# The decay rows of a state-space branch in two row groups of TensorE, and four products of a constant tile at its start

## The chip, the cores and the metric

The kernel runs on one core of a Trainium2 chip. The metric is the device time of one execution in microseconds; three timed runs and one profiled execution of the kernel before are at hand. Everything is computed in fp32.

## The reference, cut to what matters

A first block (state-space mixer and differential attention side by side, then a convolutional feed-forward) is followed by a second block of two layers. Each layer of the second block normalizes its input, projects it, sends slices of the projection through four branches and projects their joined outputs back. One of the four branches is a state-space model with a scalar decay for each of four heads:

```python
def ssd_branch(xbc, dt_raw, z, conv_w, conv_b, dt_bias, a_log, d_skip, norm_g):
    ...
    dt = jax.nn.softplus(dt_raw.astype(f32) + dt_bias.astype(f32))
    a = (dt * (-jnp.exp(a_log.astype(f32)))).reshape(bsz, nc, CHUNK, C_GROUPS, e)
    ...
    a_cs = jnp.cumsum(a, axis=2)
    xdt = xs * dt[..., None]
    ...
    seg = a_cs[:, :, :, None] - a_cs[:, :, None, :]
    lmat = masked_exp(causal, seg)
    cb = jnp.einsum('bclgn,bcsgn->bclsg', cm, bm)
    scores = cb[..., None] * lmat
    y_diag = jnp.einsum('bclsge,bcsgep->bclgep', scores, xdt)
    wx = xdt * jnp.exp(a_cs[:, :, -1:] - a_cs)[..., None]
    states = jnp.einsum('bclgn,bclgep->bcgepn', bm, wx)
    ...
```

`dt` and the running sum `a_cs` are thus four rows (one for a head) of 512 positions. Each has to be spread over 128 partitions, since it multiplies whole tiles. The first thing that the whole program does is the norm of the first block: the sum of squares over 1024 channels for each of 528 positions, in two halves of 264.

## The kernel before, in words

The kernel is one hand-written program: each engine has its instruction list in the order in which it runs, and the engines wait for each other by semaphores. Activations lie with channels on partitions and positions along the free dimension. Weights stream through a ring of four slots of 512 KB (`ring`), loaded by SyncE as slots become free. PSUM has eight banks, `bank(0)` to `bank(7)`; in the second block `take(b)` lets PE wait until bank b was released, and `full(b)` on ScalarE or `got(b)` on VectorE waits until it was written.

**The start.** ScalarE squares the input channel tile by tile (L1477). PE sums the squares over partitions by products with a matrix of ones (`norm_sum`, L491): four tiles alone, and one tile into which VectorE has added the other four (`squares_half`, L2233). ScalarE makes the inverse root (L1479, L1480), VectorE scales the input with it (`norm_half`, L2241), and each scaled tile releases a product of the first projection (`proj_half`, L510). The order on PE is norm_sum(0), proj_half(0, 0), proj_half(1, 0), norm_sum(1), and so on. VectorE writes some small constants at its start (L2190 to L2193); the last of these raises `eps_ready`, for which ScalarE waits before its first table load (L1455). PE waits only for its constants (`ones_in`, L500) and its data.

**The decay rows.** One weight slot of each layer, `misc`, has the four columns for `dt` in columns 0 to 3. So the projection leaves `dt_raw` on partitions 0 to 3 of a tile. VectorE adds the bias and takes the absolute value (L2785, L2786), ScalarE does exponential and logarithm (L1903 to L1905), VectorE finishes the softplus, multiplies by the decay rate and takes the running sum (L2793 to L2796). The results are `DT4`, which is `POSF[0:4]`, and `AC4`, which is `R[0:4]`. All of that runs early in the layer.

**Spreading them.** Much later in the layer, behind the last attention head, comes this order on PE (L1322 on): `c_decay`, `late(22, 0, 1)`, `c_cols`, `b_states`, `c_turn(10)`, `late(22, 2, 3)`, `c_turn(12)` and so on. `c_decay` makes four products, one for a head, with `sel4` as the stationary operand: four rows, of which one is 1, so that row h of `AC4` comes out on all 128 partitions of bank 2 + h. ScalarE turns each bank into two tiles and a column (L2004 to L2006). `c_cols` transposes the four rows of `DT4` and `AC4`, eight tiles of 4 x 128 into one bank, and ScalarE copies the 32 columns (L2009); VectorE needs them in `c_seg` (L3001). `late(j, x)` (L969) is a part of a projection: four products of 256 columns for each x, into one of two banks.

In the trace each fp32 product is two records of weight load and two of product.

Of the kernel before, what the change touches and what calls it, by code (L numbers as in the profile page):

```python
# [69 lines left out]
BANK = {name: i % 4 for i, name in enumerate(PHASE1)}  # L70
BANK |= {"km": 1, "k1": 3, "nk2": 2, "nk3": 3, "y0": 0, "y1": 3, "y2": 3, "y3": 3}

MAGIC = 12582912.0
# [76 lines left out]
def build(nc, a, out):  # L150

    with ExitStack() as ctx:
# [200 lines left out]
        KRR = R[:, 0:SEQ]  # L353
        AC4 = R[0:4, 0:SEQ]
        DT4 = POSF[0:4, :]
        ACB, EAB, DD = QF, SD, QF
# [28 lines left out]
        def bank(b):  # L385

            return PS[b // 2][:, b % 2, :]
# [73 lines left out]
        def _(pe):  # L461
# [33 lines left out]
            def chunk_in(b):  # L495

                s, value = n.now("hn_ready")
                pe.wait_ge(s, value - (KD - 1 - b))

            pe.wait_ge(SEMS["ones_in"], 16)  # L500

# [36 lines left out]
            def s5_out(a):  # L538
# [8 lines left out]
                ins.then_inc(SEMS[f"act_full{p}"], 1)  # L547

            norm_sum(0)
            proj_half(0, 0)  # L550
            proj_half(1, 0)
# [379 lines left out]
            for l in range(LAYERS):  # L931
# [211 lines left out]
                def c_decay():  # L1143
                    pe.wait_ge(*n("c_mul"))
                    for h in range(4):
                        take(2 + h)
                        mm(bank(2 + h), c("sel4", h * P, P, 4), AC4[0:4, :], start=True, stop=True).then_inc(SEMS[f"ba{2 + h}"], 1)

                def c_cols():
                    take(7)  # L1150
                    for t in range(4):
                        for x in range(2):
                            ins = nc.tensor.transpose(bank(7)[:, t * 8 + 4 * x:t * 8 + 4 * x + 4], (DT4, AC4)[x][0:4, t * P:t * P + P],
                                                      c("ident", 0, 4, 4))
                    ins.then_inc(SEMS["ba7"], 1)
# [282 lines left out]
        def _(act):  # L1438
# [338 lines left out]
            for l in range(LAYERS):  # L1777
# [124 lines left out]
                act.wait_ge(*n("c_dve"))  # L1902
                step(af(R[0:4, 0:SEQ], R[0:4, 0:SEQ], ACT.Exp, scale=-1.0))  # L1903
                af(LB2[0:4, 0:1], v2(l, "alog", rows=4), ACT.Exp)
                af(R[0:4, 0:SEQ], R[0:4, 0:SEQ], ACT.Ln, bias=epsc[0:4, 2:3]).then_inc(SEMS["c_act"], 1)  # L1905
                swapped()
# [101 lines left out]
                full(7)  # L2008
                released(af(COL.rearrange("p a b -> p (a b)"), bank(7)[:, 0:32], ACT.Copy), 7)  # L2009
                mark("c_acb")  # L2010
# [158 lines left out]
        def _(dve):  # L2169
# [17 lines left out]
            def join():  # L2187
                link(dve.drain())

            v.memset(epsc[:, 0:1], EPS)  # L2190
            v.memset(epsc[:, 1:2], 1e-5)
# [586 lines left out]
            for l in range(LAYERS):  # L2778
# [5 lines left out]
                dve.wait_ge(*n("d_misc"))  # L2784
                link(ts(DT4, PJ2[0:4, 16, :], v2(l, "dtb", rows=4), None, ALU.add))  # L2785
                stt(R[0:4, 0:SEQ], DT4, -1.0, DT4, ALU.mult, ALU.max).then_inc(SEMS["c_dve"], 1)  # L2786
                dve.wait_ge(*n("d_root"))
# [4 lines left out]
                dve.wait_ge(*n("c_act"))  # L2792
                link(stt(DT4, DT4, 0.0, R[0:4, 0:SEQ], ALU.max, ALU.add))  # L2793
                link(ts(LB2[0:4, 0:1], LB2[0:4, 0:1], -1.0, None, ALU.mult))
                link(ts(AC4, DT4, LB2[0:4, 0:1], None, ALU.mult))
                v.tensor_tensor_scan(AC4, c("keep", 0, SEQ, 4), AC4, 0.0, ALU.mult, ALU.add).then_inc(SEMS["c_mul"], 1)  # L2796

# [477 lines left out]
def layout(x):  # L3275
# [20 lines left out]
    for l in range(LAYERS):  # L3296
        w2 = f["w_in_2"][l]
        two = lambda o: [chunks(w2, s) for s in slices(o, 2)]
        misc = np.zeros((D, P), np.float32)
        misc[:, 0:4] = w2[:, c0 + 768:c0 + 772]  # L3300
        misc[:, 64:96] = w2[:, c0 + 1412:c0 + 1444]
        misc[:, 96:128] = misc[:, 64:96][:, swap]
        slots += two(c0 + 1028) + [chunks(w2, slice(c0 + 1284, c0 + 1412)), chunks(misc, slice(0, P))]
        for o in (0, 256, P, 256 + P):
            slots.append(chunks(w2, slice(o, o + P)))
        for o in (3 * 256 + 256, 3 * 256, 3 * 256 + 512):
            slots += two(o)
        slots += [chunks(w2, s) for s in slices(c0, 6)]
        for o in (c0 + 772, c0 + 1444, 6 * 256, 512):
            slots += two(o)  # L3310
        wo2 = f["w_out_2"][l].reshape(4, 256, D)[[2, 0, 1, 3]].reshape(D, D)
        slots += [chunks(wo2, s) for s in slices(0, 8)]
# [14 lines left out]
    def cols(v):  # L3327
        return v.reshape(-1, P).T
# [14 lines left out]
    for k in range(4):  # L3343
        sel4[k, k] = 1.0
    invf = np.zeros((P, 1))
# [4 lines left out]
    for i in range(4):  # L3350
        for q in range(64):
            b, m = q >> i, 1 << i
            lvl[2 * m * b:2 * m * b + m, i, q] = 1.0
    small, par2 = [], []
    for l in range(LAYERS):
        qb = f["d_qb_w_2"][l].reshape(2, P, 4, QKR)
# [6 lines left out]
            "lbl": cols(f["b_lb_logits_2"].reshape(-1)), "bng": cols(f["b_norm_g_2"][l]), "ccw": cols(f["c_conv_w_2"][l].reshape(-1)),  # L3363
            "ccb": cols(f["c_conv_b_2"][l]), "dtb": f["c_dt_bias_2"][l][:, None], "alog": f["c_a_log_2"][l][:, None],
            "dsk": cols(np.repeat(f["c_d_2"][l], 64)), "cng": cols(f["c_norm_g_2"][l]), "qag": cols(f["d_qa_g_2"][l]),
# [30 lines left out]
```

## Time and profile before

| | |
|---|---|
| timed runs | 1502.93, 1503.41, 1507.72 us; median 1503.41 |
| the profiled execution's own time | 1503.56 us |
| its span, first to last instruction | 1501.80 us |
| mean granted clock of TensorE | 0.996 |
| PE busy / weight loads / VectorE / ScalarE / GpSimd | 98% / 73% / 63% / 30% / 6% of the span |
| chain that ended last, by engine | PE 89%, VectorE 8%, issue 1% |
| DMA | 120.10 MB, mean 80 GB/s |

The page gives busy time by engine, the span in slices, the chain of work that ended last (followed back from the last instruction, at each step to what released it) and the costliest groups of instructions. Narrower views list instructions in order of time, the busy time of each engine in a chosen stretch with the granted clock, or one source line. A busy share says nothing by itself where stages have different limits, so the stretches that the change touches are looked at alone.

### The profile page before, as it was taken

To read this page: it belongs to the slowest core of one execution; us is meant where nothing else is said; L and a number is where in the kernel's file an instruction comes from. 1 tells how busy PE (TensorE), PEld (TensorE's weight loads), DVE (VectorE), ACT (ScalarE), POOL (GpSimd) and SP (SyncE) were. 2 spreads that over 40 slices of the span, in tenths; PEclk is the share of its full clock that TensorE was granted. 3 is DMA by queue.
4 is the path that set the end of the run, shared out by engine and by line. 5 is a ranking of instruction groups with operands and counts; after the bars stand their busy time and mean duration, and the time that the engine had idled before them with its cause. 6 is when DMAs were issued, how large, how long until landed. Compare 5 with 4: busy or idle time off the path is not lost.

```text
span 1501.8 us, 18758 instructions
## 1 busy us (share of the span) xinstructions
PE 1472.8 (98%) x7228; PEld 1091.7 (73%) x7228; DVE 952.9 (63%) x1657; ACT 449.3 (30%) x929; POOL 97.2 (6%) x70
## 2 busy tenths in 40 slices
PE   7999999999999999999999999999999999999997
PEld 6886777888888888888888844555867745456855
DVE  5849476623777666777634268877743577876833
ACT  3674444530121111111100242134443342243432
POOL 0252000000000000000000051000000150000000
PEclk9999999999999999999999999999999999999999
DMA  5211111142212222222222321112132311111132
GB/s 215 84 43 57 57 57 57 57 164 80 75 69 97 84 84 85 84 85 84 87 96 98 113 70 57 57 43 84 43 127 71 127 47 65 45 54 43 57 126 70
DMA packets 38297, 120.10 MB, mean 80 GB/s; under 512 B 4000, under 2 KB 8352, under 8 KB 37696
## 3 DMA queue, kind: packets, MB, share of 16 engines
q1 hardware_dynamic: 37872, 116.66, 22.9%
q0 software_dynamic: 336, 2.23, 0.4%
q8 instruction: 58, 0.95, 0.3%
q14 instruction: 31, 0.25, 0.1%
HBM read 112.58 MB, written 6.29 MB: 79 GB/s over the span
## 4 chain that ended last, share of the span: by engine, by line
PE 89%; DVE 8%; issue 1%; DVEq 1%; DMA 0%; ACT 0%; SPq 0%; ACTq 0%
PE PS L844 19%; PE PS L941 14%; PE PS L911 9%; PE PS L969 5%; PE PS L521 5%; PE PS L664 5%; PE PS L1217 4%; PE PS L788 4%; PE PS L1360 4%; PE PS L1387 3%; PE PS L510 2%; PE PS L620 2%; DVE SC L2804 1%; PE PS L1018 1%; PE PS L758 1%
## 5 line engine op out<-in xcount | busy, mean ns | idle before, releaser
L941 PE MATMUL PS<-HN,ring 128*128 128x512 f32 x576 | 258.0, 595 | 0.0
L941 PEld LDWEIGHTS PS<-HN,ring 128*128 128x128 f32 x576 | 107.0, 190 | 121.1 <-issue 118.8
L844 PE MATMUL PS<-SC 128*128 128x257 f32 x624 | 144.1, 380 | 3.6 <-DVEq L2185 3.5
L1722 ACT ACTIVATE SC<-PS 128x257 f32<-128x257 f32 x60 | 23.1, 385 | 374.8 <-PE PS L844 296.6
L844 PEld LDWEIGHTS PS<-SC 128*128 128x128 f32 x624 | 118.1, 190 | 21.8 <-DVEq L2185 4.8
L2804 DVE SCALAR_TENSOR_TENSOR SC<-SC 128x512 f32<-128x512 f32 x120 | 109.7, 914 | 5.4
L844 PE MATMUL PS<-HN,ring 128*128 128x257 f32 x352 | 79.8, 380 | 0.0
L844 PEld LDWEIGHTS PS<-HN,ring 128*128 128x128 f32 x352 | 66.8, 190 | 9.5
L521 PE MATMUL PS<-HN,ring 128*128 128x257 f32 (+1 forms) x320 | 71.6, 383 | 0.0
L521 PEld LDWEIGHTS PS<-HN,ring 128*128 128x128 f32 x320 | 60.4, 190 | 10.1 <-issue 1.1
L1217 PE MATMUL PS<-HN,ring 128*128 128x256 f32 x256 | 56.4, 380 | 0.0
L1387 PE MATMUL PS<-PJ,ring 128*128 128x256 f32 (+2 forms) x256 | 56.2, 380 | 0.0
L788 PE MATMUL PS<-PJ,ring 128*128 128x257 f32 x256 | 55.6, 380 | 0.0
L2493 DVE TENSOR_TENSOR SC<-ring 128x512 f32<-128x512 f32 x37 | 25.6, 693 | 47.2 <-DMA ring<-wst 41.2
L1360 PE MATMUL PS<-PJ,ring 128*128 128x512 f32 x128 | 55.3, 592 | 0.0
L911 PE MATMUL PS<-PJ,SC 128*128 128x256 f32 x240 | 54.7, 379 | 0.0
L1217 PEld LDWEIGHTS PS<-HN,ring 128*128 128x128 f32 x256 | 48.5, 190 | 7.2 <-issue 0.7
L788 PEld LDWEIGHTS PS<-PJ,ring 128*128 128x128 f32 x256 | 48.5, 190 | 6.9
L1387 PEld LDWEIGHTS PS<-PJ,ring 128*128 128x128 f32 x256 | 43.9, 190 | 13.0 <-issue 1.0
L911 PEld LDWEIGHTS PS<-PJ,SC 128*128 128x128 f32 x240 | 45.6, 190 | 6.2
L844 PE MATMUL PS<-SC,ring 128*128 128x257 f32 x208 | 49.4, 379 | 0.0
L3195 DVE TENSOR_TENSOR PJ<-PJ 128x512 f32<-128x512 f32 (+3 forms) x18 | 9.2, 514 | 62.5 <-ACT PJ L2058 62.3
(563 smaller groups left out, 2667.7 us busy)
## 6 DMA issues: line engine op xcount, KB each, us to landing
ring<-wst SPq DMA_DIRECT2D x188, 512.0 KB, 3.7
outT<-X SPq DMA_DIRECT2D x18, 256.0 KB, 4.4
X<-xT SPq DMA_DIRECT2D x16, 264.0 KB, 5.5
X<-outT SPq DMA_DIRECT2D x16, 256.0 KB, 4.8
V<-small POOLq DMA_DIRECT2D x2, 1024.0 KB, 6.6
outT<-X SPq DMA_DIRECT2D x4, 384.0 KB, 2.6
V<-s5w SPq DMA_DIRECT2D x1, 1280.0 KB, 10.5
consts<-cst SPq DMA_DIRECT2D x1, 1235.5 KB, 12.9
```

The source lines that it names most:

```text
L510: ins = mm(PS[p][:, h, 0:H], ring[:, j, b * P:b * P + P], HN[:, b, HX[h]], start=(b == 0), stop=(b == KD - 1))
L521: ins = mm(PS[p][:, h, 0:q.stop - q.start], ring[:, k % 4, b * P:b * P + P], HN[:, b, q], start=(b == 0), stop=(b == KD - 1))
L664: ins = mm(PS[at % 2][:, 1, 0:257], left[:, b * P:b * P + P], right[:, b, :], start=(b == 0), stop=(b == 3))
L788: ins = mm(PS[p][:, h, 0:257], ring[:, s, (4 * x + b) * P:(4 * x + b) * P + P], src, start=(b == 0), stop=(b == 3))
L844: ins = mm(PS[at % 8 // 2][:, at % 2, 0:257], left[:, b * P:b * P + P], right[:, b, :], start=(b == 0), stop=(b == 3))
L911: ins = mm(PS[at % 8 // 2][:, at % 2, 0:256], left, right, start=(b == 0), stop=(b == KH - 1))
L941: ins = mm(bank(b), ring[:, r, i * P:i * P + P], HN[:, i, 0:SEQ], start=(i == 0), stop=(i == KD - 1))
L969: ins = mm(bank(b)[:, 0:256], left[x][:, k * P:k * P + P], right[x][:, k, :], start=(k == 0), stop=(k == 3))
L1217: ins = mm(bank(in_bank(l, j))[:, 0:256], ring[:, j, x * P:x * P + P], HN[:, x, HF[h]], start=(x == 0), stop=(x == KD - 1))
L1360: ins = mm(bank(out_bank(l, i)), ring[:, j % WSLOTS, b * P:b * P + P], PJ2[:, src, :], start=(x == 0), stop=(x == KD - 1))
L1387: ins = mm(bank(out_bank(l, i))[:, 0:q.stop - q.start], ring[:, j % WSLOTS, b * P:b * P + P], PJ2[:, src, q], start=(x == 0), stop=(x == K ...
L2804: link(stt(CA[:, cc, :], x, w1, CA[:, cc, :], ALU.mult, ALU.add))
```

## The change

Four things are done.

- `sel4`, the `dt` columns of `misc`, the bias and the decay rate are laid out so that the four heads lie on rows 0, 1, 32 and 33 (`DTROW`) instead of 0 to 3; `DT4` and `AC4` have 34 rows, of which 30 hold zeros or values that nobody uses. The operations of VectorE and ScalarE on them take 34 partitions.
- `c_decay` goes through the heads in the order 0, 2, 1, 3. Each product takes two rows, 0-1 for heads 0 and 1 and 32-33 for heads 2 and 3.
- `c_cols` transposes tiles of 34 x 128 with a 34 x 34 identity; ScalarE picks the eight wanted columns of each head pair in two copies.
- VectorE first fills 512 columns of a tile with 1.0. PE, as soon as `eps_ready` is raised, multiplies that tile with itself three times (128 x 128 by 128 x 512, into bank 7, nobody reads it) before it waits for its constants, and once more between norm_sum(0) and proj_half(0, 0).

```diff
+DTROW = [0, 1, 32, 33]
+NDT = 34
...
-        AC4 = R[0:4, 0:SEQ]
-        DT4 = POSF[0:4, :]
+        AC4 = R[0:NDT, 0:SEQ]
+        DT4 = POSF[0:NDT, :]
...
+            pe.wait_ge(SEMS["eps_ready"], 1)
+            for _ in range(3):
+                mm(PS[3][:, 1, :], BB[:, 0, 0, :], BB[:, 0, 0:4, :], start=True, stop=True)
             pe.wait_ge(SEMS["ones_in"], 16)
...
+            def warm(n_):
+
+                for _ in range(n_):
+                    mm(PS[3][:, 1, :], BB[:, 0, 0, :], BB[:, 0, 0:4, :], start=True, stop=True)
+
             norm_sum(0)
+            warm(1)
             proj_half(0, 0)
...
                 def c_decay():
                     pe.wait_ge(*n("c_mul"))
-                    for h in range(4):
+                    for h in (0, 2, 1, 3):
                         take(2 + h)
-                        mm(bank(2 + h), c("sel4", h * P, P, 4), AC4[0:4, :], start=True, stop=True).then_inc(SEMS[f"ba{2 + h}"], 1)
+                        rows = slice(32 * (h // 2), 32 * (h // 2) + 2)
+                        s0 = CC["sel4"][0] + h * P
+                        mm(bank(2 + h), cst[rows, s0:s0 + P], AC4[rows, :], start=True, stop=True).then_inc(SEMS[f"ba{2 + h}"], 1)
 
                 def c_cols():
                     take(7)
                     for t in range(4):
                         for x in range(2):
-                            ins = nc.tensor.transpose(bank(7)[:, t * 8 + 4 * x:t * 8 + 4 * x + 4], (DT4, AC4)[x][0:4, t * P:t * P + P],
-                                                      c("ident", 0, 4, 4))
+                            o = (2 * t + x) * NDT
+                            ins = nc.tensor.transpose(bank(7)[:, o:o + NDT], (DT4, AC4)[x][:, t * P:t * P + P], c("ident", 0, NDT, NDT))
                     ins.then_inc(SEMS["ba7"], 1)
...
-                step(af(R[0:4, 0:SEQ], R[0:4, 0:SEQ], ACT.Exp, scale=-1.0))
-                af(LB2[0:4, 0:1], v2(l, "alog", rows=4), ACT.Exp)
-                af(R[0:4, 0:SEQ], R[0:4, 0:SEQ], ACT.Ln, bias=epsc[0:4, 2:3]).then_inc(SEMS["c_act"], 1)
+                step(af(AC4, AC4, ACT.Exp, scale=-1.0))
+                af(LB2[0:NDT, 0:1], v2(l, "alog", rows=NDT), ACT.Exp)
+                af(AC4, AC4, ACT.Ln, bias=epsc[0:NDT, 2:3]).then_inc(SEMS["c_act"], 1)
...
-                released(af(COL.rearrange("p a b -> p (a b)"), bank(7)[:, 0:32], ACT.Copy), 7)
+                for g in range(2):
+                    ins = af(COL.rearrange("p t (x h) -> p (t x) h", x=2)[:, :, 2 * g:2 * g + 2],
+                             bank(7)[:, 0:8 * NDT].rearrange("p (a b) -> p a b", b=NDT)[:, :, 32 * g:32 * g + 2], ACT.Copy)
+                released(ins, 7)
...
+            v.memset(XS.rearrange("p a r n -> p (a r n)")[:, 0:512], 1.0)
             v.memset(epsc[:, 0:1], EPS)
...
-                link(ts(DT4, PJ2[0:4, 16, :], v2(l, "dtb", rows=4), None, ALU.add))
-                stt(R[0:4, 0:SEQ], DT4, -1.0, DT4, ALU.mult, ALU.max).then_inc(SEMS["c_dve"], 1)
+                link(ts(DT4, PJ2[0:NDT, 16, :], v2(l, "dtb", rows=NDT), None, ALU.add))
+                stt(AC4, DT4, -1.0, DT4, ALU.mult, ALU.max).then_inc(SEMS["c_dve"], 1)
...
-                link(ts(AC4, DT4, LB2[0:4, 0:1], None, ALU.mult))
-                v.tensor_tensor_scan(AC4, c("keep", 0, SEQ, 4), AC4, 0.0, ALU.mult, ALU.add).then_inc(SEMS["c_mul"], 1)
+                link(ts(AC4, DT4, LB2[0:NDT, 0:1], None, ALU.mult))
+                v.tensor_tensor_scan(AC4, c("keep", 0, SEQ, NDT), AC4, 0.0, ALU.mult, ALU.add).then_inc(SEMS["c_mul"], 1)
...
-        misc[:, 0:4] = w2[:, c0 + 768:c0 + 772]
+        misc[:, DTROW] = w2[:, c0 + 768:c0 + 772]
...
-        sel4[k, k] = 1.0
+        sel4[DTROW[k], k] = 1.0
```

## Rows read from the trace of the kernel before

**Rows 1.** The page, part 4: the chain that ended last, by engine.
```profile
PE 89%; DVE 8%; issue 1%; DVEq 1%; DMA 0%; ACT 0%; SPq 0%; ACTq 0%
```

**Rows 2.** Stretches: us, busy time (instructions) of PE, PEld, DVE, ACT, POOL; clock; DMA.
```profile
1044.20:1047.80 3.60, 3.60 (x9) 1.40 (x8) 1.13 (x2) 3.37 (x9) 0.00 (x0) 1.00 0.27 112
...
1048.70:1052.10 3.40, 3.40 (x10) 2.66 (x9) 0.00 (x0) 1.63 (x5) 0.00 (x0) 0.50 0.46 154
...
1379.80:1383.20 3.40, 3.40 (x10) 2.69 (x9) 0.00 (x0) 1.83 (x6) 0.00 (x0) 0.50 0.47 154
...
1291.10:1294.50 3.40, 1.79 (x6) 0.51 (x5) 3.12 (x8) 1.99 (x5) 0.00 (x0) 1.00 0.01 2
...
318.90:321.70 2.80, 2.80 (x21) 2.20 (x21) 0.69 (x1) 2.38 (x6) 0.00 (x0) 1.00 0.32 126
```

**Rows 3.** The chain of waits, 1030 to 1075 us: start, us, what.
```profile
1044.30 3.62 PE PS L1147 x8
1047.93 5.34 PE PS L969 x16
1053.26 0.59 PE PS L1153 x8
...
1055.72 3.46 PE PS L969 x16
1059.18 0.87 PE PS L1162 x8
```

**Rows 4.** The start in order of time: start, us, instruction, count [idle before, releaser].
```profile
3.82 0.21 ACT L1473 ACTIVATE SC<-params 128x16 f32<-128x16 f32 x1 [1.55 <-DMA params<-par]
...
6.70 4.62 PE L491 MATMUL PS<-HN,consts 128*128 128x264 f32 x10 [6.70 <-ACT HN L1477]
...
10.03 0.66 PEld L491 LDWEIGHTS PS<-HN,consts 128*128 128x128 f32 x2 [0.22 <-DVEq L2185]
...
10.69 0.60 DVE L2215 SCALAR_TENSOR_TENSOR SC<-SC 128x16 f32<-128x16 f32 x3
...
13.09 7.14 PE L510 MATMUL PS<-HN,ring 128*128 128x264 f32 x31 [1.76 <-DVE HN L2241]
...
20.28 2.39 PE L491 MATMUL PS<-HN,consts 128*128 128x264 f32 x10
```

**Rows 5.** PE in order of time, 186 to 194 us, attention scores of the first block.
```profile
186.90 0.60 PE L689 MATMUL PS<-PJ 64*128 64x400 f32 x1
186.90 0.60 PE L691 MATMUL PS<-PJ 64*128 64x400 f32 x1
...
187.77 2.00 PE L664 MATMUL PS<-X,SC 128*128 128x257 f32 x8
...
192.79 0.69 PE L684 MATMUL PS<-PJ 64*128 64x512 f32 x1
...
193.32 0.59 PE L684 MATMUL PS<-PJ 64*128 64x512 f32 x1
```

**Rows 6.** VectorE in order of time: the running sum in layer 0.
```profile
884.68 1.21 DVE L2796 TENSOR_TENSOR_SCAN R<-consts,R 4x512 f32<-4x512 f32 x1
```

**Rows 7.** ScalarE and VectorE in order of time, behind the decay products of layer 0.
```profile
1053.89 0.20 ACT L2009 ACTIVATE SC<-PS 128x32 f32<-128x32 f32 x1 [0.20 <-PE PS L1153]
...
1054.75 0.29 DVE L2872 COPY SC<-PS 128x128 f32<-128x128 f32 x1 [9.38 <-PE PS L1095]
...
1060.21 0.18 DVE L3001 TENSOR_TENSOR SC<-SC 128x16 f32<-128x16 f32 x1
```

**Rows 8.** VectorE in order of time: a one-input operation on 512 columns.
```profile
52.43 0.43 DVE L2304 TENSOR_SCALAR SC<-SC 128x512 f32<-128x512 f32 x1
```

**Rows 9.** The line of the weight loads, 0 to 14 us.
```profile
L417 SPq DMA_DIRECT2D ring<-wst x4: 467/656/706, 3.7 to 8.8; - x4
...
DMA to landing us min/median/max: 6.4/7.5/8.1
```

**Rows 10.** PE in order of time: the transposes ahead of the output projections, first block.
```profile
318.93 3.02 PE L771 MATMUL PS<-consts,SC 2*128 2x2 f32 x20
```

More of the change, by code:

```diff
@@ L2792, in _ @@
                 dve.wait_ge(*n("c_act"))
-                link(stt(DT4, DT4, 0.0, R[0:4, 0:SEQ], ALU.max, ALU.add))
-                link(ts(LB2[0:4, 0:1], LB2[0:4, 0:1], -1.0, None, ALU.mult))
-                link(ts(AC4, DT4, LB2[0:4, 0:1], None, ALU.mult))
-                v.tensor_tensor_scan(AC4, c("keep", 0, SEQ, 4), AC4, 0.0, ALU.mult, ALU.add).then_inc(SEMS["c_mul"], 1)
+                link(stt(DT4, DT4, 0.0, AC4, ALU.max, ALU.add))
+                link(ts(LB2[0:NDT, 0:1], LB2[0:NDT, 0:1], -1.0, None, ALU.mult))
+                link(ts(AC4, DT4, LB2[0:NDT, 0:1], None, ALU.mult))
+                v.tensor_tensor_scan(AC4, c("keep", 0, SEQ, NDT), AC4, 0.0, ALU.mult, ALU.add).then_inc(SEMS["c_mul"], 1)
                 def taps(cc, lo, hi):
@@ L3354, in layout, with at_rows @@
     small, par2 = [], []
+    def at_rows(v):
+        out = np.zeros((NDT, 1), np.float32)
+        out[DTROW, 0] = v
+        return out
     for l in range(LAYERS):
@@ L3363, in layout @@
             "lbl": cols(f["b_lb_logits_2"].reshape(-1)), "bng": cols(f["b_norm_g_2"][l]), "ccw": cols(f["c_conv_w_2"][l].reshape(-1)),
-            "ccb": cols(f["c_conv_b_2"][l]), "dtb": f["c_dt_bias_2"][l][:, None], "alog": f["c_a_log_2"][l][:, None],
+            "ccb": cols(f["c_conv_b_2"][l]), "dtb": at_rows(f["c_dt_bias_2"][l]), "alog": at_rows(f["c_a_log_2"][l]),
             "dsk": cols(np.repeat(f["c_d_2"][l], 64)), "cng": cols(f["c_norm_g_2"][l]), "qag": cols(f["d_qa_g_2"][l]),
```

## The prediction, made before the changed kernel was run

> **What bounds the kernel now.** I read the page first: the chain that ended last is 89% PE [rows 1]. So a microsecond counts only if it is taken out of PE's own queue, or out of one of the few waits of PE. The change touches two places, and I read a narrower view of each.
>
> The first is the decay products (L1147), once in each of the two layers of the second block. In the table by stretches [rows 2] PE is never idle there, and the granted clock falls right behind them: 1.00 during the decay products, then 0.50 (the 1.2 GHz level of the two) from 1048.7 to 1052.1. The same comes in layer 1 at 1379.8. What the engine did before each fall is the same: products that fill 4 of 128 rows. In the chain [rows 3] the eight records take 3.62 us, and the sixteen records behind them (the first two `late` products) 5.34 us, where sixteen of the same size take 3.46 us at 1055.72.
>
> The second is the start [rows 4]. The ten records of the first norm sum (L491) take 4.62 us from 6.70; the same ten take 2.39 us at 20.28. That isn't ScalarE's pace alone: the last product of the first group has its input at 10.03 and ends at 11.32. So PE is at the lower level there (0.44 us a record against 0.22); the clock's own records begin only later. ScalarE's root, VectorE's scaling and the first projection (13.09) follow that end.
>
> **The change, part by part.** All sums are against the profiled execution: 1503.56 us, a span of 1501.80 and 1.76 around it; the median of the runs is 1503.41, 0.15 less.
>
> *Decay products, two row groups.* Today eight records follow each other at 0.43 to 0.45; in the chain up to the next product it is 3.62 us [rows 3]. After the change head 0 sits on rows 0-1 and head 2 on rows 32-33, in different banks, then 1 and 3. The kernel has such pairs already: the attention scores of the first block (L689 and L691) use rows 0-63 and 64-127. Both start at 186.90 and the next product starts at 187.77 [rows 5]: two 400-column products in 0.87 us, though one 512-column product alone takes about 0.9 (two records, [rows 3]). So pairs overlap, with a wait on a bank between them too. A 512-column product of such a pair has its two records 0.53 apart (192.79, 193.32), not 0.43: I take it that the second weight load is no longer hidden. Four steps of 0.53 are 2.12, so a gain of 3.62 - 2.12 = 1.5 us a layer, **3.0 us**. Ends: four steps of 0.43 (1.72 us, gain 1.9 a layer); or eight steps of 0.53 without overlap (4.24, a loss of 0.6 a layer). I take the pair's own row because it is the same size and mode. The Trainium skill (TensorE: Matmul & The Clock Gate, Part 3, Measured speedup vs the span model) has packed tiles last as long as one product plus about 4 ns a tile; by that the four products would take two product lengths, about 1.72 us, and the time would be 0.8 us lower than mine. The 0.53 of rows 5 speaks for the longer value.
>
> *The clock behind them.* With the four products down to 2.1 us I expect no fall. 3.4 us at half clock cost 1.7 us a layer [rows 2], so **3.4 us** in all; ends 0 and the whole difference of rows 3, 5.34 - 3.46 = 1.88 a layer. What speaks for it: from 1291.1 to 1294.5 PE is busy for 1.79 of 3.40 us, so it stands still for 1.6, and the clock stays at 1.00 [rows 2]. A mostly empty array for 2.1 us is only a little more than that, so this is the least certain term.
>
> *Transposes of 34 instead of 4 rows* (c_cols). The eight take 0.59 us a layer; eight with 128 columns take 0.87 [rows 3]. Between 0 and 0.28, nearer to the small end: 0.1 a layer, **+0.2 us**.
>
> *ScalarE and VectorE.* Operations on 34 partitions instead of 4 have the same number of columns; I cost them at nothing, and the last of them (the scan, L2796) is done at 885.9 in layer 0, 158 us ahead of the products that use it [rows 6]. The copy of the columns (L2009) becomes two of 0.20 us. Its reader on VectorE comes 6.1 us later (1060.21 against 1054.09, [rows 7]), so that is covered; without the cover it would cost 0.2 a layer. The zero columns of the projection and the tables change no DMA. Reordering the four `take` waits costs nothing: in the chain PE passes all four without a gap [rows 3].
>
> *The start.* VectorE's memset of 128x512 stands ahead of `eps_ready`, for which ScalarE waits, and now PE. Nothing in the trace is that memset; a 128x512 tensor_scalar takes 0.43 [rows 8], so `eps_ready` comes 0.4 later, at about 1.4. ScalarE hides that: it is done with its table load 1.55 us before the parameters land [rows 4]. So does VectorE, whose next operation waits for the same transfer. Three 512-column products at the low level are six records of 0.44 x 512/264 = 0.85, so 5.1 us, from 1.5 to 6.6 at the latest; the first real product starts at 6.70. The cover is thin, but 0.2 us late there would cost nothing, since the sum waits for its last input until 10.03. With the clock up, that last product runs from 10.06 and ends after 0.22 + 0.39 at 10.67 instead of 11.32: **0.65 us**. VectorE is free for the scaling at 11.29 (L2215, [rows 4]), and the first weights are there by about 10.1 (issued at 3.7, 6.4 to landing, [rows 9]), so the first projection can start at 12.4. The fourth product (`warm(1)`, 0.86 us) then runs from 10.5 to 11.4, inside PE's wait for VectorE. Ends: 0 where the clock comes up too late, 0.65.
>
> *Sum:* 0.65 + 3.0 + 3.4 - 0.2 = 6.85; 1503.56 - 6.85 = **1496.7 us**, 0.45% below the median. Behind the decay, VectorE idles 9.4 us until b_states [rows 7] and moves with PE; what could be late next is ScalarE, which copies the decay banks that PE takes again in c_turn, but that is two `late` products and some transposes further on, over 5 us of PE. About 0.3% (4.5 us) is what a measurement of this kernel can tell from no change.
>
> **The rivals.**
> 1. *The clock still falls behind the shorter decay products, in both layers.* For it: 2.1 us of two or four rows is still a stretch in which the array is nearly empty, and six transposes stand just ahead. Against it: it is 1.5 us shorter, and two groups work at a time. 1496.7 + 3.4 = 1500.1. The Trainium skill (same page, Part 4: PE-mode transpose) says that transposes don't count as busy for the clock in the same way, which would make the weak stretch longer. By that 1500.1 would be the likelier; but from 318.9 to 321.7 PE does twenty transposes (L771) and nothing else to speak of, and the clock stays at 1.00 [rows 2, 10]. Chance 0.16.
> 2. *One fall is left, or a new one comes.* After the change the sum's early products take 0.22 a record, so PE idles between them and until 10.03, and it can drop to the low level as the projections begin; the wait at 1291 also meets the clock at another moment. A fall costs 1.7: 1498.4. Against it: the waits of 1.76 us ahead of 13.09 and of 1.6 at 1291 left the clock up [rows 2, 4]. Chance 0.13.
> 3. *The groups take turns* (slower): each weight load waits for the other group's product, no overlap, eight steps of 0.53. That is 0.6 a layer more, and the clock falls as now: 1503.56 + 1.2 + 0.2 - 0.65 = 1504.3; with a fall twice as long, 1507.7. The whole is slower than before as soon as the products of a layer take over 3.85 us (3.62 + half of 0.65 - 0.1) with the clock as now. Against it: rows 5. Chance 0.05.
> 4. *The change doesn't do what it says:* the four products run one after the other as now, and only the start gains: 1503.1. Chance 0.04.
>
> **How the numbers follow.** The forecast has 0.62. The range goes from 1495.2 (1.9 and 1.88 a layer for the two decay terms, no charge for the transposes, and the 0.15 by which the median lies below the profiled execution) to 1501.0 (rival 1 with nothing gained at the start and the transposes at their upper end). It leaves out rivals 3 and 4. Faster by over 0.3% (below 1498.9) is the forecast and most of rival 2: 0.72. Slower by over 0.3% is rival 3 with the longer fall and what I have not seen: 0.03. The rest, 0.25, is within 0.3%.
>
> **What would show it.** In the profile after: the eight records of the decay products within about 2.1 us and starting in pairs; the granted clock 1.00 in the stretch behind them, and its sixteen records in some 3.5 us; the last record of the first norm sum ending at about 10.7 and the first projection starting at about 12.4. The forecast is wrong if the clock still reads 0.50 behind the decay, if the pair's records follow each other, or if the first projections run at 0.44 a record.

## The result, and the profile of the changed kernel

**Faster, and by more than forecast.** The changed kernel's median is 1495.28 us over four executions (1494.77 to 1495.38). The kernel before, run beside it, gave 1504.39 (1502.93 to 1507.72). The ratio is 0.9938, 95% interval 0.9924 to 0.9953. On the median of 1503.41 that I was shown this is 1494.1 us, or 9.3 us less, where the forecast had 6.85. A second set of executions gave 1494.96 us and the same ratio [0.9926, 0.9950]. One thing stands out before any view is opened: the kernel before spreads over 5 us, the changed one over 0.6.

First the page of the changed kernel: its span, and the chain by engine, which answers to [rows 1].

```profile
span 1493.0 us, 18777 instructions
...
PE 90%; DVE 8%; issue 1%; DVEq 1%; DMA 0%; ACT 0%; SPq 0%; ACTq 0%
```

PE is still nearly the whole chain. The span is 8.8 us shorter than the 1501.80 of before. Next the table by stretches, with the columns of [rows 2]: the decay products and the two `late` products behind them, first in layer 0, then in layer 1.

```profile
1042.50:1044.46 1.96, 1.96 (x10) 0.68 (x8) 1.14 (x2) 1.73 (x5) 0.00 (x0) 1.00 0.54 226
1044.46:1048.11 3.65, 3.65 (x18) 2.96 (x16) 0.00 (x0) 3.65 (x12) 0.00 (x0) 1.00 0.41 140
1369.66:1371.60 1.94, 1.94 (x10) 0.69 (x9) 1.12 (x2) 1.71 (x5) 0.00 (x0) 1.00 0.00 0
1371.60:1375.25 3.65, 3.65 (x19) 2.96 (x17) 0.00 (x0) 3.65 (x12) 0.00 (x0) 1.00 0.44 146
```

The granted clock is 1.00 in all four; before it was 0.50 behind the decay products of both layers. The chain of waits of the changed kernel gives the lengths, as [rows 3] did.

```profile
1042.62 1.92 PE PS L1161 x8
1044.53 3.65 PE PS L981 x16
1048.18 0.62 PE PS L1168 x8
...
1050.67 3.46 PE PS L981 x16
1054.13 0.87 PE PS L1176 x8
```

Line by line against [rows 3]: the decay products (now L1161) take 1.92 instead of 3.62 us, the sixteen `late` records (L981) 3.65 instead of 5.34, the eight transposes (L1168) 0.62 instead of 0.59. The rows below them are unchanged. Last the start in order of time, as in [rows 4].

```profile
0.92 0.48 DVE L2207 MEMSET SC<- 128x512 f32 x1 [0.92 <-PEq L3413]
...
1.50 5.49 PE L505 MATMUL PS<-SC 128*128 128x512 f32 x6 [1.50 <-DVE junk L2211]
6.78 2.41 PE L494 MATMUL PS<-HN,consts 128*128 128x264 f32 x8
9.44 0.71 PE L494 MATMUL PS<-HN,consts 128*128 128x264 f32 x2 [0.25 <-DVEq L2202]
9.98 1.02 PE L558 MATMUL PS<-SC 128*128 128x512 f32 x2
11.91 2.46 PE L516 MATMUL PS<-HN,ring 128*128 128x264 f32 x10 [0.91 <-DVE HN L2259]
...
5.57 2.18 ACT L1491 ACTIVATE HN<-X 128x264 f32<-128x264 f32 x6 [1.54 <-DMA X<-xT]
```

The three early products fill 1.50 to 6.99, the fourth (L558) fills half of PE's wait, and the first projection (L516) starts at 11.91 instead of 13.09. Not all of these 1.18 us are the change's: the last row shows that the first input tile reached ScalarE at 5.57, where the profiled execution of before had 6.13. A second profile of the changed kernel (below) has 6.08 there and is the fairer one to compare.

I went along PE's instructions one by one and noted how far each is ahead of the same one before. The gains named so far came where I looked for them, but there are three more steps, of 0.13, 0.36 and 0.33 us, at 213, 439 and 1294 us, where the change touches nothing. The two larger ones come out of VectorE (so does the smallest: ahead of L2365 at 210.75 us it idled 0.52 us in the kernel before, 0.15 in the changed one). Its rows in order of time, the kernel before:

```profile
424.30 0.42 DVE L2561 SCALAR_TENSOR_TENSOR X<-PS,X 128x257 f32<-128x257 f32 x1 [0.71 <-PE PS L844]
...
1281.46 1.23 DVE L2840 TENSOR_TENSOR PJ<-PJ,SC 128x1024 f32<-128x1024 f32 x1 [0.50 <-DVE SC L2838]
...
1293.76 0.52 PE L1027 MATMUL PS<-consts,SC 128*128 128x128 f32 x3 [1.39 <-ACT PJ L1840]
```

The same instructions in the changed kernel:

```profile
422.63 0.42 DVE L2579 SCALAR_TENSOR_TENSOR X<-PS,X 128x257 f32<-128x257 f32 x1 [0.35 <-PE PS L856]
...
1276.05 1.23 DVE L2858 TENSOR_TENSOR PJ<-PJ,SC 128x1024 f32<-128x1024 f32 x1
...
1288.34 0.52 PE L1039 MATMUL PS<-consts,SC 128*128 128x128 f32 x3 [1.02 <-ACT PJ L1854]
```

Twice 0.36 us of idle time is gone from VectorE, and the chain VectorE, ScalarE, PE hands the second on: PE waits 1.02 instead of 1.39 us at L1027 of before. The experiments had to tell whether this belongs to the change or to one execution.

### The profile page after: what moved, and what is told of

Same layout as the page of the kernel before. It is cut to its first block, busy times and chain, and to the rows that moved or that the text cites. A ratio compares the mean times of both kernels' runs of the same rounds, so it can differ in the third digit from the quotient of the medians.

```text
span 1493.0 us, 18777 instructions
## 1 busy us (share of the span) xinstructions
PE 1470.7 (99%) x7236; PEld 1089.3 (73%) x7236; DVE 952.7 (64%) x1658; ACT 448.9 (30%) x931; POOL 97.1 (7%) x70
## 4 chain that ended last, share of the span: by engine, by line
PE 90%; DVE 8%; issue 1%; DVEq 1%; DMA 0%; ACT 0%; SPq 0%; ACTq 0%
PE PS L856 19%; PE PS L953 14%; PE PS L923 9%; PE PS L981 5%; PE PS L676 5%; PE PS L527 5%; PE PS L1231 4%; PE PS L800 4%; PE PS L1374 4%; PE PS L1401 3%; PE PS L516 2%; PE PS L632 2%; DVE SC L2822 1%; PE PS L1030 1%; PE PS L770 1%; PE PS L1002 1%
```

## Experiments

Times are medians; ratios stand against the kernel before, run on the same chip in the same set.

**The kernel before, again.** No edit.

> The kernel before, unchanged. The change brought about 9 us by the medians and 8.8 by the two spans, where the prediction had 6.85. Theory A (the terms were too small): this kernel comes again to 1503 to 1505 us, with the clock at 0.50 behind the decay products in both layers (about 3.4 us each), the last norm-sum input of the start near 10.0 us, and the VectorE stalls that the changed kernel lacks (0.35 us each near 424 and 1281 us) at the same places. Rival B (part of the 9 us was this execution's own): the stalls or the landing of the first input move by 0.3 us or more between executions of the same code, and about 1 us of the difference is theirs.

Measured: 1504.27 us (1501.45 to 1508.62, 12 executions), ratio 1.0008 [0.9997, 1.0018]. The table by stretches of its profile:

```profile
13.90:17.30 3.40, 3.40 (x9) 2.66 (x8) 3.19 (x13) 2.68 (x8) 0.00 (x0) 0.50 1.07 421
1048.15:1054.95 6.80, 6.80 (x14) 3.95 (x13) 0.00 (x0) 2.89 (x9) 0.00 (x0) 0.50 0.24 77
1382.65:1386.05 3.40, 3.40 (x10) 2.65 (x9) 0.00 (x0) 1.34 (x5) 0.00 (x0) 0.50 0.50 154
```

The same code lost its clock in other places: for 3.4 us in the first projections, for 6.8 us (from within the decay products on) in layer 0. VectorE's idle times sat at the same instructions as before (0.71 and 0.52 us), so rival B is wrong about the stalls. The first input reached ScalarE at 6.20 (before: 6.13); in the two profiles of the changed kernel it differs by 0.5 us (5.57 and 6.08), which is what rival B had in mind. What neither theory had: where and how long the clock falls differs between executions. I take that for much of the 5 to 7 us spread. Thirty-four more executions of the same code beside these twelve had a median of 1503.27, so medians of this kernel can lie 1 us apart.

**The row groups alone.**

```diff
-            v.memset(XS.rearrange("p a r n -> p (a r n)")[:, 0:512], 1.0)
...
-            for _ in range(3):
-                mm(PS[3][:, 1, :], BB[:, 0, 0, :], BB[:, 0, 0:4, :], start=True, stop=True)
...
-            warm(1)
```

> The changed kernel without its start: no memset of the constant tile, none of the four products of it; the decay rows stay in two row groups. Theory A (the parts add up): decay products in 1.9 us, the clock at 1.00 behind them in both layers, the first projection at 12.5 to 13.1 us as in the kernel before, so 2 x (1.72 + 1.69 - 0.03) = 6.8 us less than before, ratio 0.9955. Rival C (the clock stays up later only because it came up early): the clock falls behind the decay again, and the gain is 3.4 us, ratio 0.9977.

Measured: 1498.41 us (1496.22 to 1501.51), ratio 0.9961 [0.9949, 0.9972]: 4.9 us less, not 6.8. The profile has both decay gains: the eight records in 1.93 us, the clock at 1.00 behind them in both layers. Rival C is out. But there is a new fall. Stretches, then PE in order of time:

```profile
1043.97:1045.90 1.93, 1.93 (x10) 0.68 (x8) 1.14 (x2) 1.70 (x5) 0.00 (x0) 1.00 0.52 217
1045.95:1049.60 3.65, 3.65 (x19) 2.96 (x17) 0.00 (x0) 3.65 (x12) 0.00 (x0) 1.00 0.42 141
1291.80:1295.15 3.35, 3.35 (x5) 1.35 (x4) 3.21 (x7) 0.00 (x0) 0.00 (x0) 0.50 0.02 5
```
```profile
1290.16 0.52 PE L1030 MATMUL PS<-consts,SC 128*128 128x128 f32 x3 [1.36 <-ACT PJ L1845]
1291.05 0.63 PE L1037 MATMUL PS<-SC,PJ 128*128 128x64 f32 x4 [0.38 <-DVE SC L2830]
1291.52 5.35 PE L944 MATMUL PS<-HN,ring 128*128 128x512 f32 x8
```

The eight records of L944 take 5.35 us. With the clock up the same eight took 3.65 in the changed kernel:

```profile
1289.70 3.65 PE L953 MATMUL PS<-HN,ring 128*128 128x512 f32 x8
```

This is my rival 2, at the wait it named. The wait ahead of it is the long one (1.36 us).

**The start alone.** The kernel before with the memset and the four products, decay rows as they were.

```diff
+            v.memset(XS.rearrange("p a r n -> p (a r n)")[:, 0:512], 1.0)
...
+            for _ in range(3):
+                mm(PS[3][:, 1, :], BB[:, 0, 0, :], BB[:, 0, 0:4, :], start=True, stop=True)
...
+            warm(1)
```

> The kernel before with the memset and the four products of the constant tile alone; decay rows as before. Theory A: both falls of the clock stay, the decay products take 3.6 us, and the first projection starts 0.6 us earlier for the clock, up to 1.2 where the input also lands early: 0.6 to 1.2 us less, ratio 0.9992 to 0.9996, which the runs can hardly tell from none. Rival C: the falls behind the decay go too, and the gain is above 4 us. Rival D (the products at the start do harm or nothing): first projection at 13.0 us or later.

Measured: 1502.19 us (1500.51 to 1505.46), ratio 0.9990 [0.9978, 1.0001]. Falls behind both decays stay, 6.8 us each in this profile. PE at the start:

```profile
10.04 0.71 PE L491 MATMUL PS<-HN,consts 128*128 128x264 f32 x2 [1.57 <-DVEq L2194]
10.59 1.02 PE L555 MATMUL PS<-SC 128*128 128x512 f32 x2
12.52 1.80 PE L513 MATMUL PS<-HN,ring 128*128 128x264 f32 x7 [0.91 <-DVE HN L2251]
```

With the last input at 10.04 (before: 10.03) the projection starts at 12.52, 0.57 us earlier: that is the clock's part, as forecast. Theory A; rivals C and D are out. And the profile shows VectorE's 0.36 us idle times at the places of the changed kernel, though no decay row was moved.

**Four serial products, split.** The kernel before; the first `late` product stands between heads 1 and 2.

```diff
-                c_decay()
-                late(22, 0, 1)
+                c_decay(0)
+                late(22, 0)
+                c_decay(2)
+                late(22, 1)
```

> The kernel before with its four decay products split: heads 0 and 1, the first late product (four full 256-column products), heads 2 and 3, the second late product. Four rows each, one after the other, no row groups. Theory A1 (the fall comes from the unbroken stretch of nearly empty products): no fall in either layer, the eight records cost their 3.6 us a layer all the same, 3.4 us less than before, ratio 0.9978. Rival A2 (any such products pull the clock down, and the row groups themselves keep it up): the clock falls as before, time within 1 us of before, or more where both halves pull it down.

Measured: 1502.26 us (1500.86 to 1504.42), ratio 0.9996 [0.9986, 1.0005]. By the times this is inconclusive. The profile is not:

```profile
1044.26 1.98 PE L1148 MATMUL PS<-R,consts 4*128 4x512 f32 x4
1046.17 1.99 PE L969 MATMUL PS<-HN,ring 128*128 128x256 f32 x8
1048.09 1.98 PE L1148 MATMUL PS<-R,consts 4*128 4x512 f32 x4
1050.00 1.99 PE L969 MATMUL PS<-HN,ring 128*128 128x256 f32 x8
```

No fall in either layer. From the first decay record to the first transpose it is 7.66 us (1044.26 to 1051.92) instead of 8.96 (3.62 + 5.34, [rows 3]). I suspected that the start hid the gain in the times, and tried the split again with the start in place.

**The split with the start.** The edits of the two kernels above together.

```diff
+                c_decay(0)
+                late(22, 0)
+                c_decay(2)
+                late(22, 1)
...
+            warm(1)
```

> The kernel before with the whole start of the change, and its four serial decay products split by the first late product, as in the earlier run; there the profile had no fall, but the times spread over 3.6 us and the median was only 1.0 us less. Theory A1 (no fall behind split products, and the spread there was the late rise of the clock at the start): no fall in the profile, two halves of 1.91 us where the changed kernel has 1.91 in all, so 2 x 1.91 more than the changed kernel, 1498.8 us, spread under 1.5 us, ratio 0.9968. Rival A2 (the clock falls behind split products in most executions): 1500 to 1502 us, with a spread of 1.7 us or more.

Measured: 1499.54 us (1499.18 to 1500.30, 10 executions), ratio 0.9965 [0.9953, 0.9977]. The spread is 1.1 us, and both stretches hold their clock:

```profile
1043.22:1051.00 7.78, 7.78 (x26) 4.28 (x26) 1.14 (x2) 7.03 (x19) 0.00 (x0) 1.00 0.32 120
1372.43:1380.20 7.77, 7.77 (x27) 4.25 (x25) 1.15 (x2) 7.05 (x19) 0.00 (x0) 1.00 0.20 70
```

Theory A1 holds, 0.7 us above its time: in the four instances of the two split kernels, two halves of 1.9 us with full products between them kept the clock, without row groups. So it is the unbroken run of such products that the falls follow, not such a product as such. But not every run of few rows loses the clock: the twenty transposes of [rows 10], two rows for 3.0 us, had no fall behind them in any profile, and no run here shows what separates the two kinds of run. Against the kernel with the start alone the split is worth 2.65 us (1502.19 - 1499.54) without any row group. The changed kernel remains 4.3 to 4.6 us ahead, twice 2.10 of it here: from the first decay record to the first transpose the split takes 7.67 us (1043.26 to 1050.93), the changed kernel 5.57 (1042.55 to 1048.12).

**The changed kernel, again.** No edit.

> The changed kernel, unchanged. The kernel before comes in anywhere between 1501.4 and 1508.8 us, and in the two profiles of it the clock falls in different places. Theory A: the changed kernel has almost no stretch left in which the clock can fall, so it stays within about 1 us of 1495.3 and its profile shows no fall before the last 10 us. Rival B (the first four executions were lucky): it spreads over 1495 to 1500 us, with a fall of 3.4 us or more in some executions, at the wait near 1291 us for one, as in the kernel with the row groups alone.

Measured: 1494.96 us (1494.92 to 1495.23), ratio 0.9938 [0.9926, 0.9950], no fall before 1490.11 us. Theory A holds, rival B is out. PE at the start:

```profile
1.50 4.72 PE L505 MATMUL PS<-SC 128*128 128x512 f32 x6 [1.50 <-DVE junk L2211]
6.65 2.02 PE L494 MATMUL PS<-HN,consts 128*128 128x264 f32 x8 [0.44 <-ACT HN L1491]
9.83 0.71 PE L494 MATMUL PS<-HN,consts 128*128 128x264 f32 x2 [1.16 <-DVEq L2202]
10.38 1.02 PE L558 MATMUL PS<-SC 128*128 128x512 f32 x2
12.31 7.36 PE L516 MATMUL PS<-HN,ring 128*128 128x264 f32 x32 [0.90 <-DVE HN L2259]
```

**Neighbours in one row group.**

```diff
-                    for h in (0, 2, 1, 3):
+                    for h in (0, 1, 2, 3):
```

> The changed kernel with the heads taken as 0, 1, 2, 3: two neighbours in one row group follow each other, and only heads 1 and 2 can overlap. Theory A (it is the overlap of two row groups that shortens the decay products): the eight records take 1.91 + 0.86 = 2.8 us where the changed kernel has 1.91, at most one overlap left, 1.7 us more in the two layers, about 1497.0, ratio to before 0.996; the clock may fall behind them in some executions, 1.7 us each. Rival E (the order does not matter, the engine sorts the groups out): 1.9 us as in the changed kernel, and the same time.

Measured: 1495.43 us (1494.96 to 1495.61), ratio 0.9940 [0.9928, 0.9952]. Theory A was wrong and rival E right. PE in order of time:

```profile
1043.22 1.99 PE L1161 MATMUL PS<-R,consts 2*128 2x512 f32 x8
1045.14 3.72 PE L981 MATMUL PS<-HN,ring 128*128 128x256 f32 x16
```

The next work starts 1.92 us after the first record, as in the changed kernel. The single records still start in pairs, now 13 ns apart instead of 7. Heads 0 and 1 share rows, and products in the same rows followed each other in the kernel before, so head 2 must have started beside head 0, ahead of head 1. The semaphores that the records carry say so directly: those of heads 0 and 2 are on the records that start at 1043.75 and 1043.76, those of heads 1 and 3 on the ones at 1044.61 and 1044.62. But they rise in program order: heads 0, 1, 2, 3 at 1044.35, 1045.21, 1045.25, 1045.30, head 2 behind head 1 and 0.90 us behind head 0, beside which it ran. The reordered loop of the change is worth nothing here; the two row groups are.

**The changed kernel without the four products, memset kept.**

```diff
-            for _ in range(3):
-                mm(PS[3][:, 1, :], BB[:, 0, 0, :], BB[:, 0, 0:4, :], start=True, stop=True)
...
-            warm(1)
```

> The changed kernel with the memset kept and the four products of the constant tile left out. In the traces so far VectorE has idle times of 0.36 us at fixed instructions, and in both kernels with the memset they sit at other instructions than in those without: 0.71 against 0.35 ahead of the product copy at 424 us, 0.50 against 0.14 ahead of the mask at 1281 us. PE is 0.84 us earlier for it in all (0.13 at 212, 0.36 at 439, 0.35 at 1291 us). Theory F (one more VectorE instruction moves them): this kernel is 0.8 us faster than the row groups alone, 1497.6 us by its median, with the stalls at the places of the changed kernel and the first projection at 12.9. Rival G (they come with the products or the earlier start): the stalls are at the places of the kernel before, and the time that of the row groups alone, 1498.4.

Measured: 1496.26 us (1495.49 to 1498.81), ratio 0.9949 [0.9936, 0.9962]. VectorE's idle times are at the places of the changed kernel (0.36 us ahead of the copy, none ahead of the mask), and PE waits 1.02 us near 1292: theory F. The time is 2.1 us below the row groups alone, where theory F had 0.8; the fall at 1291 us of that one is a candidate for the rest, not shown. The profile is of the slowest of its executions, and shows what the four products are for:

```profile
6.40 4.86 PE L494 MATMUL PS<-HN,consts 128*128 128x264 f32 x10 [6.40 <-ACT HN L1482]
13.03 10.26 PE L513 MATMUL PS<-HN,ring 128*128 128x264 f32 x32 [1.77 <-DVE HN L2250]
```

Thirty-two projection records take 10.26 us instead of 7.36: the clock came up only at 18.91.

**One VectorE instruction more, in the kernel before.**

```diff
+            v.memset(XS.rearrange("p a r n -> p (a r n)")[:, 0:1], 1.0)
             v.memset(epsc[:, 0:1], EPS)
```

> The kernel before with one VectorE instruction more ahead of its first: a memset of one column of a tile that nobody reads before it is written. Nothing else changes. Theory F: the 0.36 us idle times of VectorE move as with the large memset (0.35 ahead of the copy at 424, 0.14 ahead of the mask at 1281), PE is 0.8 us earlier by 1291 us, and the time is 0.8 us less, ratio 0.9995, within what the runs can tell. Rival G: no idle time moves, no difference along the sequence of PE.

Measured: 1502.43 us (1500.38 to 1505.49), ratio 0.9989 [0.9977, 1.0001]; the times can't tell. The rows can:

```profile
425.45 0.43 DVE L2562 SCALAR_TENSOR_TENSOR X<-PS,X 128x257 f32<-128x257 f32 x1 [0.36 <-PE PS L844]
...
1280.58 1.23 DVE L2841 TENSOR_TENSOR PJ<-PJ,SC 128x1024 f32<-128x1024 f32 x1
```

Along PE's sequence it gains 0.16, 0.37 and 0.37 us at the three places, 0.90 in all, with one tiny instruction that nobody needs. Theory F is shown: idle times of 0.36 us sit at VectorE instructions that are fixed by how many stand ahead of them. The count can be read from the trace: of VectorE's records (2419 in the kernel before, those of its sequencer included) the ones that gained an idle time of this size were, with two exceptions, numbers 574, 958, 1086, 1214, 1598, 2238 and 2366, and one further on with the extra instruction; they lie whole multiples of 128 apart. The clock of this profile came up at 16.25, which cost 1.44 us; behind the decay products of layer 0 it did not fall, which gave 1.67 back.

**The changed kernel with one VectorE instruction more.**

```diff
+            v.memset(XS.rearrange("p a r n -> p (a r n)")[:, 512:513], 1.0)
             v.memset(XS.rearrange("p a r n -> p (a r n)")[:, 0:512], 1.0)
```

> The changed kernel with one more VectorE instruction at its head, a memset of one column. Theory F (VectorE's idle times of 0.36 us sit at a place that is counted in instructions): they move again, each loss or gain is 0.36 us at most where PE waits for VectorE, and which it is I cannot tell beforehand; 1494.3 to 1496.0 us. Rival K (it was the first memset's time, not the count): no idle time moves, 1495.0 to 1495.3.

Measured: 1495.19 us (1494.80 to 1495.30), ratio 0.9938 [0.9923, 0.9952]. At some sixteen instructions an idle time of 0.3 to 0.36 us came or went, the two that matter to PE stayed short, and the time stayed. It moves them (F), with no gain left in it.

**Which of the four products?** First without the one ahead of the projection.

```diff
             norm_sum(0)
-            warm(1)
             proj_half(0, 0)
```

> The changed kernel without the fourth product, the one between the first norm sum and the first projection. PE then stands still for some 1.7 us ahead of the projection, as in the kernel before, and a second run of that one showed the clock fall from 13.9 to 17.3 us behind such a wait. Theory A: the first projection starts when it does in the changed kernel (12.0 to 12.6), the best executions are as fast, and in some the clock falls in the first projections: median 1495.0 to 1496.5, highest near 1497. Rival H (three early products are enough): 1495.0 with the same spread of under 1 us.

Measured: 1497.03 us (1495.10 to 1498.05), ratio 0.9950 [0.9935, 0.9965]. A stretch and PE's order of time:

```profile
11.40:18.20 6.80, 6.04 (x14) 4.74 (x15) 6.34 (x20) 2.94 (x8) 0.00 (x0) 0.50 1.06 407
```
```profile
12.16 10.35 PE L516 MATMUL PS<-HN,ring 128*128 128x264 f32 x32 [1.76 <-DVE HN L2258]
```

The clock was up at 4.56 and fell again behind the waits. Five of six executions lie 1.8 us or more above the best. Theory A, with a larger loss than I expected. Then the fourth product alone:

```diff
-            for _ in range(3):
-                mm(PS[3][:, 1, :], BB[:, 0, 0, :], BB[:, 0, 0:4, :], start=True, stop=True)
...
             norm_sum(0)
             warm(1)
```

> The changed kernel with the fourth product alone, without the three ahead of the first norm sum. Without any of the four the clock came up between 10.5 and 18.9 us in six profiles, and a late rise cost up to 3 us in the first projections; the median of that kernel was 1496.3. Theory A: the norm sum runs at 0.44 us a record, the first projection starts near 12.9, and the one product fills the wait but cannot bring the clock up by itself: 1495.6 to 1498.5, median near 1496. Rival J (the product in the gap is what counts): under 1495.5, and the clock up by 12 us in every execution.

Measured: 1495.70 us (1495.17 to 1496.90), ratio 0.9942 [0.9928, 0.9957].

```profile
5.99 3.47 PE L494 MATMUL PS<-HN,consts 128*128 128x264 f32 x8 [5.99 <-ACT HN L1489]
...
13.06 7.36 PE L514 MATMUL PS<-HN,ring 128*128 128x264 f32 x32 [0.91 <-DVE HN L2257]
```

By time, norm sum and first projection it is theory A, and J's 1495.5 is missed by 0.2. But the projections run at full clock, and not by the fourth product alone: the clock came up at 8.92, within the norm sum, before that product ran, so whether it could bring the clock up stays open. By the medians the fourth product is worth 1.7 to 2.1 us (1497.03 against 1494.96 and 1495.28), the first three 0.4 to 0.7.

## Why the prediction fell short

The direction and the mechanisms of the forecast's terms were right; two gains were sized too small, and one was not in the sum. The second profile of the changed kernel (span 1493.4, first input at 6.08) is the like-for-like partner of the profiled execution of before. Its 8.4 us, by how far PE is ahead along its sequence:

| term | forecast | measured |
|---|---|---|
| start | 0.65 | 0.78 (0.2 of it the last input, at 9.83 instead of 10.03) |
| decay products, two layers | 3.0 | 3.4 (1.70 + 1.71) |
| clock fall behind them | 3.4 | 3.4 (1.69 + 1.68) |
| transposes | -0.2 | -0.06 |
| VectorE's idle times | not in the sum | 0.8 (0.13 + 0.36 + 0.33) |
| sum | 6.85 | 8.4 (the terms give 8.3; 0.04 lies in small steps) |

**The step that failed most** is the one on the memset. I wrote that "`eps_ready` comes 0.4 later" and "ScalarE hides that", that is, a cost and its cover, and excluded a gain. What one instruction more does to the 1657 behind it wasn't in the sum. It moved the 0.36 us idle times, and 0.8 us of them came off PE's waits. That is over half of the shortfall in this pair of profiles. It is luck and no merit of the change: in the kernel before, one small memset that nobody needs did the same, and one instruction more in the changed kernel moved idle times again without a gain. It was not to be read from one trace of before: a single profile shows such an idle time as a wait for PE or for VectorE's own last result ("0.71 <-PE PS L844"), and only a second kernel shows that it moves.

**"Four steps of 0.53 are 2.12"** was mis-sized. The records of the changed kernel start 0.53, 0.43, 0.43 and 0.52 us apart: 1.91. The 0.53 of [rows 5] is the first step of a run. My reason for it, a second weight load that isn't hidden, was wrong: it is the first one, whose record starts together with the first product's (1044.23 and 1044.23 before), and that product's record is 0.69 us long where the others have 0.59. The decay products of before have it too, once (1044.23 to 1044.76), and I could have seen that their 3.62 us are eight steps of 0.43 and 0.18 for the ends. The Trainium skill (TensorE: Matmul & The Clock Gate, Part 3, Measured speedup vs the span model) gave an estimated 1.72 for the four; the trace has that and 0.19 for the ends, so the rule was the better half of the answer and the rows of before had the rest.

**The transposes** were rightly put near the small end, 0.03 instead of 0.1 a layer.

**The clock fall** was sized right in the profile, and rival 1 is out: in eight profiles with the two row groups the clock holds behind the decay in all sixteen instances. Unbroken serial products had a fall in seven of eight, split ones in none of four. But one profile couldn't show how long a fall lasts: in the second profile of the kernel before that of layer 0 lasted 6.8 us instead of 3.4 and cost 1.6 us more. **Rival 2** did not come in the changed kernel, but in two parts of it: at 1291 us with the groups alone, in the first projections without the fourth product. So the chance that I gave it was not too high; what kept it away was the start's other half and, perhaps, the shorter wait at L1027. The latter is argued, not shown: the fall at 1291 came in one of four profiles with the long wait, and in none of ten with the short one.

**The start** was right in its mechanism (0.57 us with the same input times) but I priced one execution. In the six profiles without any of the four products the clock came up for the first time at 10.49, 11.08, 11.56, 11.77, 16.25 and 18.91 us, and in one of them it fell again at 13.91; the last two and that fall cost 1.4 to 2.9 us in the projections. The profiled execution of before had neither. The two late ones are the two with a memset more ahead and no product; with one profile of each, whether that matters stays open. The Trainium skill (the same page, Part 1) warns that the number of slow products at a kernel's start differs between runs of the same code. The trace agrees: the two profiles of the kernel before differ by 0.6 us in the rise, those of the changed kernel by 2.4 (7.70 and 5.31). I left it out. By the medians, taking the four products away costs 1.0 to 1.3 us (1496.26 against 1495.28 and 1494.96), about twice my term. The rest of the 9.1 us between the two medians, beyond this and the other terms, fits the longer falls of the kernel before; no run separates it.

Range and chances followed from the sum: its low end took the better ends of the two decay terms alone, so a term that I had not seen was enough to reach past it.

## What to carry to other kernels

Give products that fill a few rows their own row groups, or at least break their run with full ones: here the clock that was lost behind them cost as much as the row groups took off the products themselves, 1.7 us a layer each. A wait of 1.8 us near the start is worth one idle product that keeps the clock, and the gain shows as a narrower spread as much as in one profile. When a step appears in the trace where nothing was changed, compare that engine's idle times instruction by instruction over several kernels before calling it noise.

## What was not expected of the hardware

- VectorE's idle times of about 0.36 us belong to a place in its instruction stream. Kernels with the same count of instructions ahead had them at the same instructions; one 128x1 memset more in the changed kernel moved some sixteen of them. The places lie whole multiples of 128 instructions apart in VectorE's stream, so which instruction is hit can be counted. What VectorE does there the profile doesn't name, and it stays open.
- A product whose row group is busy does not hold up the one behind it in another group (heads 0, 1, 2, 3: 1.92 us). The Trainium skill (the same page, Part 3, The mechanism) has products start and end strictly in program order; the neighbours' profile speaks against the start for products in different row groups. The semaphores of the four rose in program order all the same, as the page's "end" would have it (1044.35, 1045.21, 1045.25, 1045.30).
- A clock that is up early can be lost early: with three early products and without the fourth it was up at 4.56 us and at 0.50 from 11.39 to 18.22, and by the medians (1497.03 against 1496.26) that was no better than none of the four.
